# Four chunks of the last modulation vector leave TensorE: ScalarE products, GpSimd's accumulating DMAs, two raw weight buffers

## What is computed

```python
sh1, sc1, g1, sh2, sc2, g2 = jnp.split(silu(cond) @ w_ada + b_ada, 6)
h = rms_norm(x, g_norm1) * (1 + sc1) + sh1
q, k, v, bg, cg, u = split(h @ w_in)
attn = block_attention(rope(rms_norm(q)), rope(rms_norm(k)), v)
conv_out = bg * short_conv(cg * u, conv_w)
mixed = concat(rms_norm(attn), rms_norm(conv_out))
x = x + g1 * (mixed @ w_out)
h2 = rms_norm(x, g_norm2) * (1 + sc2) + sh2
x = x + g2 * ec_moe(h2, w_router, w_gate, w_up, w_down)   # 16 experts, top 2*T/16 tokens each
```

## Time and profile before

| | |
|---|---|
| median of three runs | 1523.64 us |
| the profiled execution, whole | 1525.6 us |
| its span, first to last instruction | 1523.9 us |
| PE busy | 1447.1 us (95%) |
| DVE, ACT, POOL busy | 602.1, 254.9, 26.8 us |
| bytes read from HBM | 565.02 MB |

### The profile page before, as it was taken

One profiled execution on the slowest core, in us unless ns is written; L12 is line 12 of the kernel. 1 busy time (PEld: TensorE's weight loads), 2 busy tenths in 40 slices (PEclk: granted clock), 3 DMA queues, 4 the chain that ended last, 5 costly groups with the idle time before them and its releaser, 6 DMA issues.

```text
span 1523.9 us, 18531 instructions
## 1 busy us (share of the span) xinstructions
PE 1447.1 (95%) x7846; PEld 880.9 (58%) x7846; DVE 602.1 (40%) x1019; ACT 254.9 (17%) x358; POOL 26.8 (2%) x58
## 2 busy tenths in 40 slices
PE   6999999999999999999989999999889889899998
PEld 3667788888889997435435335335335335335433
DVE  5434977878768986101301301301301301211313
ACT  4223223333234223000000000000000000000200
POOL 0000000000000000000000000000000000000000
PEclk8999999999999999999999999999999999999999
DMA  9999688777787659999999999999999999999999
GB/s 373 403 395 341 259 330 305 276 260 258 279 292 269 222 188 375 368 434 432 429 433 429 433 432 431 432 431 433 432 431 433 431 432 433 430 432 428 430 423 351
DMA packets 99263, 572.48 MB, mean 376 GB/s; under 512 B 9532, under 2 KB 54532, under 8 KB 76676
## 3 DMA queue, kind: packets, MB, share of 16 engines
q1 hardware_dynamic: 87824, 520.14, 83.7%
q0 software_dynamic: 6912, 50.33, 8.6%
q10 hardware_dynamic: 4468, 1.14, 0.3%
HBM read 565.02 MB, written 6.55 MB: 375 GB/s over the span
## 4 chain that ended last, share of the span: by engine, by line
PE 66%; DMA 25%; DVE 5%; SPq 2%; issue 2%; ACT 0%; DVEq 0%
PE psum L639 64%; DMA ring<-in_w_up 20%; DMA ring<-in_w_ada 3%; SPq L551 2%; DMA res<-in_w_ada 1%; DVE res L1618 1%; DMA ring<-in_w_down 1%; DVE w_parts L1508 1%; PE psum L649 0%; PE psum L825 0%; PE psum L1077 0%; DVE stat L1578 0%; DVE hid L1577 0%; PE psum L1047 0%; DVE mix L1580 0%
## 5 line engine op out<-in xcount | busy, mean ns | idle before, releaser
L639 PE MATMUL psum<-ring,hid 128*64 128x512 f32 x3024 | 681.0, 598 | 52.9 <-DMA ring<-in_w_up 39.7
L639 PEld LDWEIGHTS psum<-ring,hid 128*64 128x64 f32 x3024 | 241.0, 138 | 469.5 <-issue 414.1
L1944 DVE TENSOR_TENSOR hid<-psum,hid 128x512 f32<-128x512 f32 x16 | 11.1, 692 | 517.1 <-PE psum L639 517.1
L639 PE MATMUL psum<-h_parts,w_parts 128*128 128x384 f32 x1152 | 207.3, 337 | 1.7 <-DVE mix L1651 1.7
L639 PEld LDWEIGHTS psum<-h_parts,w_parts 128*128 128x128 f32 x1152 | 199.9, 188 | 5.5 <-issue 2.5
L1508 DVE TENSOR_TENSOR w_parts<-ring,w_parts 128x2048 fp32r<-128x2048 f32 x52 | 119.0, 2289 | 76.0 <-ACT w_parts L1208 75.8
L1208 ACT ACTIVATE w_parts<-ring 128x2048 fp32r<-128x2048 f32 x52 | 99.6, 1915 | 210.4 <-PE psum L639 180.8
L639 PE MATMUL psum<-w_parts,h_parts 128*128 128x512 f32 x432 | 103.6, 395 | 1.3 <-DVE h_parts L1552 1.3
L639 PE MATMUL psum<-ring,early 128*32 128x512 f32 (+4 forms) x694 | 98.1, 545 | 7.0 <-DMA ring<-in_w_ada 6.0
L639 PEld LDWEIGHTS psum<-w_parts,h_parts 128*128 128x128 f32 x432 | 79.6, 188 | 26.6 <-issue 10.3
L639 PEld LDWEIGHTS psum<-early,mix 128*128 128x128 f32 x768 | 86.6, 192 | 9.0 <-issue 9.0
(11 more groups left out here) (216 smaller groups left out, 748.9 us busy)
## 6 DMA issues: line engine op xcount, KB each, us to landing
ring<-in_w_up SPq DMA_DIRECT2D x30, 4096.0 KB, 23.2
ring<-in_w_gate SPq DMA_DIRECT2D x28, 4096.0 KB, 29.8
ring<-in_w_down SPq DMA_DIRECT2D x26, 4096.0 KB, 30.0
ring<-in_w_ada POOLq DMA_DIRECT2D x48, 1024.0 KB, 7.0
ring<-in_w_in SPq DMA_DIRECT2D x36, 1024.0 KB, 8.1
ring<-in_w_ada SPq DMA_DIRECT2D x28, 768.0 KB, 15.5
res<-in_w_ada SPq DMA_DIRECT2D x16, 1024.0 KB, 6.4
ring<-in_w_out SPq DMA_DIRECT2D x16, 1024.0 KB, 5.6
```

Of the source, the lines that this page charges most:

```text
L639: return nc.tensor.matmul(out, lhsT, rhs, start=start, stop=stop, skip_group_check=True)
L1944: tt(by_row, bank[1][:, :].rearrange("p (b a) -> p a b", a=4), by_row, ALU.mult).then_inc(act_ready, 1)
```

## The change

`RAW` becomes 2, so a unit's load waits for `lo_part` of unit u-2, and the two buffers fill slot 0. SP's chunk loads of modulation 3, the row moves and the return of x move from `s - 4` to `s - 3`. The four chunks of modulation 5 are no longer PE's. Each is worked in two halves of 1024 columns, eight jobs in all: POOL loads the half (`carry_load`), ACT makes two products of it (one for each condition; `CARRY_AT`, every third s), POOL adds both to `carry_sums` in DRAM by a DMA that accumulates (`carry_add`; the first chunk's is a plain write). SP brings the sums back into `added_up` at s = 27, and DVE goes on adding the 12 other chunks to them. POOL's program is written out instead of looped.

```diff
@@ -49,7 +49,7 @@
 BLK = 512
 UC = 256
 UNIT = 8 * UC
-RAW = 3
+RAW = 2
 PARTS = 2
 BANK = 512
@@ -58,12 +58,11 @@
-STREAM = [2, 4, 5]
-HERE = 4
...
+STREAM = [2, 4]
...
 SETS_Q = [(14, 2)]
 SETS_KV = [(1, 3), (3, 2)]
...
 ORDER = [2, 4, 3, 5]
@@ -71,9 +70,15 @@
 CONV_SUMS = 21
 X_PARTS = 6
 X_PART = KC * T // X_PARTS
-ADDED = range(HERE, KC)
+CARRIED = 4
+HALF = D // 2
+CARRY_JOBS = [(k, half) for k in range(CARRIED) for half in range(2)]
+CARRY_AT = {3 * n + 1: n for n in range(len(CARRY_JOBS))}
+CARRY_LOADS = {2: 0, 5: 1, 7: 2, 9: 3, 11: 4, 13: 5, 15: 6}
+CARRY_ADDS = {4: 0, 6: 1, 8: 2, 10: 3, 12: 4, 14: 5, 17: 6}
+ADDED = range(CARRIED, KC)
 ADDS_AT = {s: 2 for s in (3, 4, 5, 7, 8, 9, 10, 11, 12, 13)} | {2: 1, 14: 3}
-ADA_USES = 2 * KC + HERE + 1
+ADA_USES = 2 * KC + 1
 BLOCKS = [(0, 768), (768, 768), (1536, 512)]
@@ -167,7 +172,7 @@
         def parts_at(name, n, at):
             return nc.alloc_sbuf_tensor_at(name, [P, n], F32R, offset=at)
...
         w_parts = parts_at("w_parts", PARTS * 2 * UNIT, ring_at + 4 * RAW * UNIT)
         h_parts = parts_at("h_parts", 2 * KC * T, ring_at + 4 * 4 * SLOT)
         attn_parts = parts_at("attn_parts", 2 * AC * T, hid_at)
@@ -248,6 +253,8 @@
         added_up = [ring[:, 6, 0:D], ring[:, 6, D:2 * D]]
         added_up_3 = [res[:, 0:D], res[:, D:2 * D]]
         chunk_3 = res[:, 2 * D:3 * D]
+        carry_in_buf, carry_out_buf = ring[:, 3, 0:HALF], ring[:, 3, HALF:2 * HALF]
+        carry_sums = nc.dram_tensor("carry_sums", (2, P, D), F32).ap()
         x_copy = nc.dram_tensor("x_copy", (X_PARTS, P, X_PART), F32).ap()
         sq2, ssum2 = sq, ssum[0]
@@ -340,6 +347,7 @@
         ada_free = sem("ada_free")
         ones_set, add_done = sem("ones_set"), sem("add_done")
         x_saved, x_back, chunk_in, add_done_3, summed_3 = sem("x_saved"), sem("x_back"), sem("chunk_in"), sem("add_done_3"), sem("summed_3")
+        carry_in, carry_ready, carry_added, carried_back = sem("carry_in"), sem("carry_ready"), sem("carry_added"), sem("carried_back")
         moe_landed = [sem(f"moe_landed{n}") for n in range(WIDE)]
         tail_landed = [[sem(f"tail_landed{n}_{half}") for half in range(2)] for n in range(len(TAIL))]
         full_landed = [sem(f"full_landed{n}") for n in range(2 * FULL)]
@@ -512,12 +520,16 @@
                     chunk_load(0)
                 if s in FIRST_AT:
                     sp.wait_ge(unit_used, U_QKV + U_CONV)
+                    if s == min(FIRST_AT):
+                        sp.wait_ge(carry_added, 32 * len(CARRY_JOBS))
+                        for n in range(2):
+                            sp.dma_start(added_up[n], carry_sums[n]).then_inc(carried_back, 16)
                     first_load(FIRST_AT[s])
-                if s - 4 in CONV_ADDS[:-1]:
-                    chunk_load(CONV_ADDS.index(s - 4) + 1)
-                if s - 4 == 19:
+                if s - 3 in CONV_ADDS[:-1]:
+                    chunk_load(CONV_ADDS.index(s - 3) + 1)
+                if s - 3 == 19:
                     perm_move(4)
-                if s - 4 == CONV_SUMS + 1:
+                if s - 3 == CONV_SUMS + 1:
                     sp.wait_ge(summed_3, 1)
                     sp.dma_start(res[:, :].rearrange("p (n t) -> p n t", n=X_PARTS), x_copy.rearrange("n p t -> p n t")).then_inc(x_back, 16)
                     perm_move(3)
@@ -615,20 +627,53 @@
             nc.gpsimd.memset(add_rows_of[:, 1:2], 1.0).then_inc(ones_set, 1)
             nc.gpsimd.memset(add_rows_of[:, 2:33], 0.0).then_inc(ones_set, 1)
             pool.wait_ge(w_used, len(PIECES))
-            def ada_load(m, k, j, added=False):
-
-                if added:
+            def ada_load(m, k):
+                j = k % 2
+                if k - 2 in ADDED and m == N_MOD - 1:
                     pool.wait_ge(add_done, 2 * (k - 2 - ADDED[0]) + 2)
+                elif m == N_MOD - 1:
+                    pool.wait_ge(ada_free, k - ADDED[0] + 2 * KC + 1)
                 else:
                     pool.wait_ge(ada_free, k + (KC * STREAM.index(m) + 1))
-                pool.dma_start(ada_buf[j], ada_rows[bass.ds(k * P, P), m * D:(m + 1) * D]).then_inc(ada_landed[j], 16)
-
-            for m in STREAM[:-1]:
-                with pool.Fori(0, KC // 2) as i:
-                    for j in range(2):
-                        ada_load(m, 2 * i + j, j)
-            for k in range(KC):
-                ada_load(N_MOD - 1, k, k % 2, k - 2 in ADDED)
+                pool.dma_start(ada_buf[j], ada_rows[k * P:(k + 1) * P, m * D:(m + 1) * D]).then_inc(ada_landed[j], 16)
+
+            def carry_add(job):
+
+                k, half = CARRY_JOBS[job]
+                pool.wait_ge(carry_ready, job + 1)
+                for n, rows in enumerate((carry_out_buf, carry_in_buf)):
+                    sums = carry_sums[n][:, half * HALF:(half + 1) * HALF]
+                    if k == 0:
+                        pool.dma_start(sums, rows).then_inc(carry_added, 16)
+                    else:
+                        pool.dma_start(sums, rows, accum_op=ALU.add).then_inc(carry_added, 16)
+
+            def carry_load(job):
+
+                k, half = CARRY_JOBS[job]
+                if job:
+                    pool.wait_ge(carry_added, 32 * job)
+                at = (N_MOD - 1) * D + half * HALF
+                pool.dma_start(carry_in_buf, ada_rows[k * P:(k + 1) * P, at:at + HALF]).then_inc(carry_in, 16)
+
+            for k in range(2):
+                ada_load(STREAM[0], k)
+            for place, events in enumerate(EVENT_SETS):
+                for m, k in events:
+                    if k < KC:
+                        t = KC * STREAM.index(m) + k + 2
+                        if t < 2 * KC:
+                            ada_load(STREAM[t // KC], t % KC)
+                        else:
+                            ada_load(N_MOD - 1, ADDED[t - 2 * KC])
+                if place in CARRY_ADDS:
+                    carry_add(CARRY_ADDS[place])
+                if place in CARRY_LOADS:
+                    carry_load(CARRY_LOADS[place])
+            carry_load(len(CARRY_JOBS) - 1)
+            carry_add(len(CARRY_JOBS) - 1)
+            for k in ADDED[2:]:
+                ada_load(N_MOD - 1, k)
             pool.wait_ge(unit_used, U_ALL - 1)
             nc.gpsimd.memset(aff2, -1.0).then_inc(padded, 1)
@@ -967,7 +1012,8 @@
             last.then_inc(aff_turned, 1)
             turn_groups(range(5, 12), rows_src, rows_banks, rows_turned, rows_free)
             pe.wait_ge(add_done, 2 * len(ADDED))
-            partition_sums(bank[0], added_up, False, ada_free)
+            pe.wait_ge(mod_read, N_MOD - 3)
+            partition_sums(bank[0], added_up, True, ada_free)
             pe.wait_ge(rows_out, 8)
             pe.wait_ge(rank_ready, 1)
             for h in range(2):
@@ -1361,6 +1407,12 @@
                 if s and s % 6 == 0:
                     csq(s // 3 - 2)
                     csq(s // 3 - 1)
+                if s in CARRY_AT:
+                    job = CARRY_AT[s]
+                    k = CARRY_JOBS[job][0]
+                    a.wait_ge(carry_in, 16 * (job + 1))
+                    nc.scalar.activation(carry_out_buf, carry_in_buf, ACT.Copy, scale=cond[:, k, 0:1])
+                    nc.scalar.activation(carry_in_buf, carry_in_buf, ACT.Copy, scale=cond[:, k, 1:2]).then_inc(carry_ready, 1)
                 if s == ATT_END + 1:
                     root(ssum[0])
@@ -1804,14 +1856,13 @@
             def ada_add(count):
                 for i in range(adds[0], adds[0] + count):
                     k, n = ADDED[i // 2], i % 2
-                    t = 2 * KC + k
+                    t = 2 * KC + k - ADDED[0]
                     v.wait_ge(ada_landed[t % 2], 16 * (t // 2 + 1))
                     if i < 2:
-                        v.wait_ge(unit_used, U_QKV + U_CONV)
-                        ts(added_up[n], ada_buf[t % 2], cond[:, k, n:n + 1], None, ALU.mult).then_inc(add_done, 1)
+                        v.wait_ge(carried_back, 32)
                     else:
                         v.wait_ge(add_done, i - 1)
-                        stt(added_up[n], ada_buf[t % 2], cond[:, k, n:n + 1], added_up[n], ALU.mult, ALU.add).then_inc(add_done, 1)
+                    stt(added_up[n], ada_buf[t % 2], cond[:, k, n:n + 1], added_up[n], ALU.mult, ALU.add).then_inc(add_done, 1)
                 adds[0] += count
             for s in range(1, U_OUT + 1):
```

More of the change, by code:

```diff
@@ L57 @@
 COLS = [(0, T_CTX), (T_CTX, T)]
-STREAM = [2, 4, 5]
-HERE = 4
-EVENT_SETS = [[(m, k) for k in range(first, min(first + 2, KC + 1))] for m in STREAM for first in range(0, KC + 1 if m < N_MOD - 1 else HERE, 2)]
+STREAM = [2, 4]
+EVENT_SETS = [[(m, k) for k in range(first, min(first + 2, KC + 1))] for m in STREAM for first in range(0, KC + 1, 2)]
 SETS_Q = [(14, 2)]
 SETS_KV = [(1, 3), (3, 2)]
-SETS_CONV = {s: 3 + n for n, s in enumerate([0, 1, 3, 4, 6, 7, 9, 10, 12, 13, 15, 16, 17, 18, 19, 21, 23])}
```

(3 more changed lines are left out.)

## The result

The changed kernel takes 1531.64 us, the median of four runs (1530.40 to 1534.95), beside 1523.99 us of the kernel before: a ratio of 1.0047, interval 1.0035 to 1.0059. It is slower by 7.7 us as medians and 7.2 us by the ratio. Five later runs gave 1531.44 us beside 1525.08, 1.0045 (1.0031 to 1.0060). The prediction was 1522.3 us with a range up to 1527.0, and "slower" had a chance of 14%. It was wrong, and on the wrong side.

The account below looks back on a forecast made before the run. PE was taken to bound the units' stage, so its work and gaps before 590 us counted; DMA bounds the experts' stage. Terms: -3.6 + 0.5 + 1.8 = -1.3 us, from 1523.64 to 1522.3 us, range 1520.0 to 1527.0.

Parts of the forecast that it names:

- PE's part: Two groups of matmuls leave PE, one at each of two places, 1.74 and 1.85 us, together 3.6 us.
- the sum said 3.1: PE's gain of 3.6 us less 0.5 us of new gap, with chunk loads not disturbed: 3.1 us faster.
- The room ahead of the convolution's outputs: First unit reading these outputs: 0.7 us of room on PE, then a new gap, taken as +0.5 us.
- I take 0.7 + 1.1 = 1.8 us: Chunk landings of modulation 3: 0.7 us later remaining in s = 4, 1.1 us in s = 5, lengthening PE's gap.
- rival 2: Accumulating packets are dear, the s = 5 chunk waiting for 8 of them: 1524.0 to 1528.5 us, chance 18%.
- the 2.4 allowed: Round of s = 3: chunk landing late by at most 2.4 us, as job 0's sums compete with a unit's load.
- POOL's waits: also 0: POOL's queue: waits for `carry_ready` and `carry_added` fit between pairs of chunk loads 10 to 13 us apart; cost 0.
- ACT: 0: ACT's 16 products, about 1.0 us each, cost 0, since DVE would not have used unit 18's top part sooner.
- Rival 3: Two raw buffers starve unit 40 or 41, unit 40 late by up to 8 us: 1524 to 1526 us, chance 10%.
- the gap of 1.68 us: Ahead of s = 6's second half: PE's only idle time for another engine between 160 and 590 us, waiting for DVE.

Follow-up runs that it names:

- 36 fillers: The changed kernel with 36 small matmuls of `ident` into an unused bank ahead of PE's wait in s = 6; 1532.92 us, ratio 1.0058.
- 20 fillers: The changed kernel with 20 small matmuls of `ident` into an unused bank ahead of PE's wait in s = 6; 1529.82 us, ratio 1.0036.

## Why the prediction was wrong

**PE's part was right.** 3.7 us left PE at the two places (3.6 forecast), and the kernel without jobs measured 3.0 us net where the sum said 3.1. The room ahead of the convolution's outputs closed where it was worked out, in the first unit that reads them: there is a gap of 0.15 us, and behind it PE is 489.34 - 484.99 = 4.35 us late against 3.54 at the start of the output projection, so 0.8 us went, where the term said 0.5. The kernel without jobs lost the same 0.8 us there (447.19 to 482.06, before 450.95 to 484.99).

**The step that failed: "I take 0.7 + 1.1 = 1.8 us" for the landings.** The gap grew by 4.2 us in the first trace and 3.5 in the second. Three things were wrong with the term.

First, it took the packets of job 1 for accumulating ones. They are plain: both first jobs belong to chunk 0. So rival 2, which was my only road to "slower" at that place, was tied to the wrong property. Making all writes plain leaves a gap of 4.81 us.

Second, the round of s = 5 was counted as an alternation packet by packet from the start, four more of POOL's packets ahead of the chunk's. The changed kernel moved 304 packets of POOL's to 17 of SP's in 5 us: all but 17 of the chunk's packets waited until 2.79 of the 3.15 MB that POOL had issued, writes included, were gone. Only then, from 243 to 246 us, did the queues move side by side (q0 96 packets, q1 137). I had read such an alternation out of the second window of the earlier trace rows, and it is not there. The same window cut in two, 239 to 240 and 240 to 242 us, in the trace of before:

```profile
q0 software_dynamic: 52, 0.37, 88.2%
q1 hardware_dynamic: 9, 0.07, 17.6%
...
q1 hardware_dynamic: 100, 0.82, 96.9%
q0 software_dynamic: 11, 0.02, 2.2%
```

The two queues stood one behind the other. By that, 1 MB more in POOL's queue costs its whole time, 2.4 us and more; the run with job 1's writes later put it at 3.7 us. The Trainium skill says in "DMA: Bandwidth & Descriptors", section "Queues, rings and completion order", that an engine takes turns between queues, but works off a whole group of some 9 to 17 descriptors of one queue before it turns. Taking a packet of the profile for one descriptor, the 304 / 16 = 19 that each engine moved for POOL are one or two turns, which the trace does not contradict; no run here shows the turns themselves.

Third, of the two places the one in s = 3 does not count. It was late by 3.5 us, more than the 2.4 allowed, yet the next landing was shorter by 1.9 and the gap with only this lateness was 1.93 us.

**The term that was missing: the clock.** The prediction priced a gap of PE at its length. Half units of s = 6 and 12 behind gaps of 0.23, 0.59, 1.45, 1.68, 1.78 and 1.93 us took 4.4 to 4.5 us; behind 2.08, 2.10, 2.47, 4.81, 5.20 and 5.85 us they took 6.02, 6.03, 6.01, 6.00, 5.80 and 7.00. The longer gaps cost 1.4 to 2.5 us on top. The length alone does not decide it: the gap of 2.44 us at s = 18 with 36 fillers left the clock at 1.00. With work in the gap that price went (4.46 us). The profile before could not show it: its gap was 1.68 us.

**The cover that was not there.** "POOL's waits: also 0" holds up to 300 us. From 320 to 420 us the DMA share is 0.93 in the changed kernel (before: 0.74), and POOL's chunks reach PE late: 1.42 us at s = 18 in the second trace, 0.82 us with plain writes. The first trace has no such wait; that its longer loss at s = 6 hides it is argued from the two traces meeting at 454.5 us. A repair at s = 6 alone gives little, because the next waits take it up: of the 2.1 us that 20 fillers gained, 1.2 went at s = 12, and the 1.39 us at s = 18 stayed. ACT's products took 1.15 us where I had put 1.0. "ACT: 0" was right for the changed kernel, but not for its variants: when a half chunk is late, ACT's wait for it holds the unit's top part and the norms, with 6.2 and 4.9 us of PE in two of the experiments.

**Rival 3 and the raw buffers.** PE lost nothing by it. Unit 40's buffer cost no time, and two buffers alone changed nothing. The one sign is that ACT waited twice for a unit's load in the changed kernel, 3.2 and 2.9 us ahead of 407.86 and 418.42 us, where between 160 and 590 us it never waited for one before; PE did not wait there.

**The baseline.** The profiled execution of before stood 2 us above the median, and I carried that difference along as if it had no place. It probably had one: the gap of 1.68 us that the whole argument started from is 2.10 us and the lower clock in an execution that took 2.4 us more, and nothing in the trace with two raw buffers. That it is absent in the faster executions of the kernel before is argued, not shown. From a start without a gap the sum of PE's lateness is (second trace of the changed kernel against that with two raw buffers): 7.0 us behind s = 6 (258.58 - 251.57; 5.2 of it the gap, 1.4 the clock, 0.4 not placed), 7.5 us ahead of the wait at s = 18, 9.2 us behind it (409.14 - 399.99), less 3.7 us, 5.5 us at the output projection (454.55 - 449.07). Another 0.8 us goes at the convolution's outputs. That is 6.3 us, where the medians of the two sets of runs are 7.7 and 6.4 us apart. The difference I leave open: from the output projection to the end, executions differ by half a microsecond and more.

## What to carry to other kernels

A transfer that an engine waits for every round must not share the DMA engines with a burst issued just ahead of it on another queue: price the burst at its whole length, not at its share. Move such a burst and look again at everything that waits on the same queue; here the same work cost 7 us less seven units later, and half of it, kept clear of the norms and of full DMA engines, was worth having. And before a gap in one profile becomes a term of a sum, look whether other executions have it, and price a longer one with the clock that it may cost.

## What the runs showed of the hardware

- The four plain writes of 0.5 MB from SBUF to DRAM by POOL's queue took 10.7 to 13.8 us to land beside other traffic. Two of them, behind 2 MB of loads on the same queue, left SP's queue 17 packets in 5 us; without them it moved 275.
- An accumulating 4 KB packet took about 0.46 us of a DMA engine in the mean, 3.3 times per byte what a plain 8 KB read took and three times what a plain 4 KB write took; by the median of the packet records it is twice the plain write.
- The granted clock fell to 1.2 GHz behind gaps of PE of 2.08 and 2.10 us, and the half unit behind them cost 1.5 us more; behind the six gaps up to 1.93 us, and behind one of 2.44 us, it stayed at 2.4 GHz.
- Identity matmuls of 128 x 128 in float32 are two records and 0.23 us each in a row, not the 0.137 us that a single record suggests (0.82 us for six of `psum<-ident,hid`).
